# Two softmax attentions in groups of four heads, transposes one head ahead, and a mixer whose branches are interleaved

## The reference, cut to what matters

```
def swa_sink_attention(h, w_q, sinks, w_out, k, v, cos, sin):      # 16 heads of 64, 4 key heads
    q = apply_partial_rope((h @ w_q)...)
    s = einsum(q, k_band) * 64 ** -0.5, -inf outside of the window of 128 keys
    m = maximum(max(s, axis=-1), sink)
    p = exp(s - m)
    probs = p / (sum(p, axis=-1) + exp(sink - m))
    return einsum(probs, v_band).reshape(...) @ w_out

def token_mixer(u, ...):
    rq, rk, rv, rg, c_q, c_kv, k_pe, gate_ret, gate_mla = split(u @ w_in)
    rq, rk = apply_rope(rq), apply_rope(rk)
    y_ret = head_norm(retention(rq, rk, rv))                         # 4 heads, 256 wide, decay by distance
    y_ret = (silu(rg) * y_ret) @ w_ret_o
    # latent attention, 8 heads of 128 + 64 (rotary)
    q = rmsnorm(c_q, q_norm) @ w_uq ;  kv = rmsnorm(c_kv, kv_norm) @ w_ukv
    y_mla = softmax_attention(q, k, v, causal) @ w_mla_o
    merged = sigmoid(gate_ret) * y_ret + sigmoid(gate_mla) * y_mla
    return merged @ w_out
```

## Time and profile before

| | |
|---|---|
| Time, median of three runs (range) | 3529.89 us (3528.61 to 3530.32) |
| The profiled execution's own time | 3529.57 us |
| Its span, first to last instruction | 3527.8 us |
| Mean granted clock of TensorE, as a share of 2.4 GHz | 0.936 |
| TensorE busy | 3154.2 us (89% of the span) |
| VectorE, ScalarE, GpSimd busy | 55%, 47%, 38% |
| Chain that ended last, by engine | PE 45%, issue 28%, DVE 13%, POOL 6%, ACT 6% |
| Weight loads: issue to landing | 3.3 us for 512 KB (882 of them) |

### The profile page before, as it was taken

How to read it: one execution, slowest core, us unless ns; L and a number is a source line. 1 busy time by engine, 2 the same in 40 slices (tenths; PEclk the granted TensorE clock), 3 DMA queues, 4 the chain that set the end, 5 groups by cost and what they waited for, 6 DMA issues and landing times.

```text
span 3527.8 us, 58527 instructions
## 1 busy us (share of the span) xinstructions
PE 3154.2 (89%) x18424; PEld 2797.6 (79%) x18424; DVE 1928.8 (55%) x3054; ACT 1657.1 (47%) x3123; POOL 1337.3 (38%) x1068
## 2 busy tenths in 40 slices
PE   6957999996999987789999779999898788999998
PEld 6756898995777775679999767777777677999997
DVE  7342634019899973234700799999302214555565
ACT  1112576779544441237767874444312214555554
POOL 7200588886455530019978755555000000000000
PEclk6888999999999998699999999999999887999999
DMA  6412454540677742134445128877342222555553
GB/s 222 153 50 93 148 173 161 179 161 0 219 256 256 258 162 84 42 121 171 169 166 184 60 84 279 256 257 242 120 155 95 96 96 84 185 184 186 185 187 132
DMA packets 154591, 556.49 MB, mean 158 GB/s; under 512 B 17024, under 2 KB 19840, under 8 KB 154384
## 3 DMA queue, kind: packets, MB, share of 16 engines
q1 hardware_dynamic: 152288, 551.62, 46.4%
q10 hardware_dynamic: 2224, 3.87, 0.3%
HBM read 554.37 MB, written 1.05 MB: 157 GB/s over the span
## 4 chain that ended last, share of the span: by engine, by line
PE 45%; issue 28%; DVE 13%; POOL 6%; ACT 6%; ACTq 1%; DVEq 1%; POOLq 0%; PEldq 0%
PE bank L634 15%; PE bank L907 11%; PE bank L447 7%; PE bank L925 5%; POOL w_parts L2098 4%; DVE a_parts L1794 4%; PE bank L660 3%; DVE w_parts L1791 3%; ACT hT L1209 3%; DVE h_parts L1791 2%; DVE mean L1802 2%; DVE hT L1802 2%; ACT hT L1205 1%; POOL arena L2137 1%; PE bank L889 1%
## 5 line engine op out<-in xcount | busy, mean ns | idle before, releaser
L2098 POOL TENSOR_TENSOR w_parts<-ring,w_parts 128x512 fp32r<-128x512 f32 x512 | 686.8, 1369 | 646.9 <-ACT w_parts L1169 643.4
L634 PE MATMUL bank<-h_parts,w_parts 128*128 128x256 f32 x6144 | 747.4, 284 | 25.0 <-POOL w_parts L2098 23.0
L634 PEld LDWEIGHTS bank<-h_parts,w_parts 128*128 128x128 f32 x6144 | 743.3, 193 | 29.3 <-POOL w_parts L2098 26.4
L1169 ACT ACTIVATE w_parts<-ring 128x512 fp32r<-128x512 f32 x512 | 319.0, 630 | 196.8 <-PE bank L634 178.1
L2049 DVE TENSOR_TENSOR w_parts<-ring,w_parts 128x512 fp32r<-128x512 f32 x384 | 265.2, 692 | 245.3 <-ACT w_parts L1336 237.3
L660 PE MATMUL bank<-w_parts,a_parts 128*128 128x512 f32 x1536 | 371.8, 398 | 17.1 <-DVE a_parts L1794 17.1
L447 PE MATMUL bank<-hT,ring 128*128 128x256 f32 x1584 | 357.4, 390 | 28.4 <-ACT hT L1100 28.4
L660 PE MATMUL bank<-h_parts,a_parts 128*128 128x512 f32 x1536 | 367.5, 395 | 16.2 <-DVE a_parts L1794 16.2
L907 PEld LDWEIGHTS bank<-h_parts,w_parts 128*128 128x128 f32 x3072 | 375.3, 193 | 5.6 <-issue 3.3
L907 PE MATMUL bank<-h_parts,w_parts 128*128 128x256 f32 x3072 | 376.2, 284 | 2.6 <-DVE w_parts L2049 2.6
L447 PEld LDWEIGHTS bank<-hT,ring 128*128 128x128 f32 x1584 | 308.7, 196 | 77.3 <-issue 31.3
(11 more groups left out here) (310 smaller groups left out, 4294.7 us busy)
## 6 DMA issues: line engine op xcount, KB each, us to landing
ring<-stream SPq DMA_DIRECT2D x882, 512.0 KB, 3.3
arena<-stream SPq DMA_DIRECT2D x168, 512.0 KB, 4.4
arena<-consts ACTq DMA_DIRECT2D x1, 1536.0 KB, 6.1
xT<-xin ACTq DMA_DIRECT2D x1, 1024.0 KB, 5.7
out<-hT SPq DMA_DIRECT2D x4, 256.0 KB, 2.2
arena<-subk ACTq DMA_DIRECT2D x2, 128.0 KB, 2.2
arena<-consts_s ACTq DMA_DIRECT2D x1, 256.0 KB, 2.6
cst<-consts ACTq DMA_DIRECT2D x1, 196.0 KB, 2.6
```

Of the source, the lines that this page charges most:

```text
L634: mm = pe.matmul(bank[k][:, 0:T], w[:, wp, ws], h_parts[:, hp, 4 * j + q, :], start=(j == 0 and q == 0 and i == 0), stop=(j == 1 and q == ...
L1169: act.activation(w_parts[half % HALVES][:, 0, :], ring[slot_][:, j * 512:(j + 1) * 512], ACT.Copy).then_inc(sem(f"{n}_high"), 1)
L2098: pool.tensor_tensor(w[:, 1, :], ring[(base + k) % RING][:, j * 512:(j + 1) * 512], w[:, 0, :].bitcast(F32), ALU.subtract).then_inc(sem(f" ...
```

## The change

- Both attentions: the softmax runs in groups of four heads (`HG`). VectorE masks four heads, takes their maxima and signals; ScalarE takes that group's exponentials meanwhile. The scaling of the probabilities follows in a second loop of VectorE, one group after the other.
- In TensorE's loop over heads the transposes of head h+1 come ahead of the products of head h. The output copies move from VectorE to ScalarE, each behind the copy of the next head's transposes.
- Mixer: the order of the stream becomes `mla_uk`, `mla_uq`, `mla_uv`, `ret_o`. TensorE's order after gate r is: sums of squares of the latents, gate m, retention scores, `mla_uk`, retention products, `mla_uq` with the head means behind its third slot, head variances, `mla_uv`, rotations, wait for `r_yn`, `ret_o` 0 to 3, attention scores, `ret_o` 4 to 7, attention, `mla_o`, `mix_out`. The roots of cq and ckv lie between the two gates on ScalarE, and ahead of the retention scores on VectorE. VectorE multiplies `ret_o` 0 to 3 by the gate ahead of its softmax, 4 to 7 behind it.
- `merged` is made by chunks of 128 features, each behind its `mla_o`; the first `mix_out` projection waits for each chunk ahead of the product that reads it.
- `M.y` gets its own place in memory, and `M.sq` takes that of before.

The diff, cut to its core:

```diff
-    ("gate_r", 8), ("gate_m", 8), ("ret_o", 8), ("mla_uq", 6), ("mla_uk", 2), ("mla_uv", 2), ("mla_o", 8),
+    ("gate_r", 8), ("gate_m", 8), ("mla_uk", 2), ("mla_uq", 6), ("mla_uv", 2), ("ret_o", 8), ("mla_o", 8),
...
         def project(...)
+                if made is not None:
+                    pe.wait_ge(*made(q))
                 mm = pe.matmul(t[:, 0:T], w[:, q * P:(q + 1) * P], src[:, q, :], start=(q == 0), stop=(q == n - 1))
...
+        def attention_pe(pe, n, heads, vcols, vtok):
+            def turned(h):
                 pe.wait_ge(sem(f"{n}_p"), h + 1)
                 t = open_tile(f"{n}_pt{h}")
                 pe.wait_ge(free_sem(f"{n}_pt{h}"), freed(f"{n}_pt{h}") - 1)
                 for k in range(3):
                     mm = pe.transpose(t[:, k * P:(k + 1) * P], A.p[:, h, k * P:(k + 1) * P], ident)
                 mm.then_inc(full_sem(f"{n}_pt{h}"), 1)
+            def weighed(h):
                 pe.wait_ge(free_sem(f"{n}_pt{h}"), freed(f"{n}_pt{h}"))
                 t = open_tile(f"{n}_o{h}")
...
+            turned(0)
+            for h in range(1, heads):
+                turned(h)
+                weighed(h - 1)
+            weighed(heads - 1)
...
         def mix_pe(pe):
             for c in range(8):
                 project(pe, "gate_r", c, hT, f"r_gate{c}")
+            norm_pe(pe, "cq", M.sqc, 3)
+            norm_pe(pe, "ckv", M.sqk, 2)
             for c in range(8):
                 project(pe, "gate_m", c, hT, f"m_gate{c}")
...
+            pe.wait_ge(sem("r_yn"), 1)
+            for c in range(DC // 2):
+                project(pe, "ret_o", c, M.y, f"r_o{c}")
+            scores_pe(pe, "m", MH, scores)
+            for c in range(DC // 2, DC):
+                project(pe, "ret_o", c, M.y, f"r_o{c}")
+            attention_pe(pe, "m", MH, lambda h: slice(h * P, (h + 1) * P), M.vm)
...
-            pe.wait_ge(sem("merged"), 1)
-            project_norm(pe, "mix_out", M.mg, "mix", "2b")
+            project_norm(pe, "mix_out", M.mg, "mix", "2b", lambda q: (sem("merged"), q + 1))
...
+        def attention_act(act, n, heads, sinks):
+            for g in range(heads // HG):
+                act.wait_ge(sem(f"{n}_max"), g + 1)
+                gs = slice(g * HG, (g + 1) * HG)
+                if sinks:
+                    act.activation(A.m[:, :, gs], A.m[:, :, gs], ACT.Exp).then_inc(signal("w_sink"), 1)
+                    act.wait_ge(sem("w_sink"), signalled("w_sink"))
+                for h in range(g * HG, (g + 1) * HG):
...
+        def attention_copies_act(act, n, heads, outp):
+            def out(h):
+                act.wait_ge(full_sem(f"{n}_o{h}"), filled(f"{n}_o{h}"))
+                outp(h, tile_of(f"{n}_o{h}")).then_inc(free_sem(f"{n}_o{h}"), 1)
+                act.wait_ge(free_sem(f"{n}_o{h}"), freed(f"{n}_o{h}"))
             for h in range(heads):
+                if h >= 2:
+                    act.wait_ge(full_sem(f"{n}_o{h - 2}"), filled(f"{n}_o{h - 2}"))
                 copy_act(act, A.pt[:, h % 2, :], f"{n}_pt{h}", lambda t: t[:, 0:384])
+                if h:
+                    out(h - 1)
+            out(heads - 1)
...
         def mix_act(act):
             for c in range(8):
                 copy_act(act, M.gr[:, c, :], f"r_gate{c}", func=ACT.Sigmoid)
+            root_act(act, "cq", rs[:, :])
+            root_act(act, "ckv", G2.r2)
             for c in range(8):
                 copy_act(act, M.gm[:, c, :], f"m_gate{c}", func=ACT.Sigmoid)
+            act.wait_ge(full_sem("r_s3"), filled("r_s3"))
+            for i in range(8):
+                copy_act(act, M.kn[:, i, :], f"m_k{i}")
             for h in range(RH):
                 copy_act(act, M.y[:, 2 * h:2 * h + 2, :], f"r_y{h}", lambda t: t[:, :].rearrange("p (e t) -> p e t", e=2))
+            for i in range(10):
+                copy_act(act, M.qn[:, i, :] if i < 8 else M.qp[:, i - 8, :], f"m_q{i}")
             for h in range(RH):
                 act.wait_ge(sem("r_cent"), h + 1)
                 act.activation(M.sq[:, 2 * h:2 * h + 2, :], M.y[:, 2 * h:2 * h + 2, :], ACT.Square).then_inc(signal("r_sq"), 1)
                 act.wait_ge(sem("r_sq"), signalled("r_sq"))
+            for i in range(10, 12):
+                copy_act(act, M.qp[:, i - 8, :], f"m_q{i}")
             root_act(act, "r", M.r)
...
+        def softmax_dve(dve, n, heads, scale, mask, sinks):
+            for g in range(heads // HG):
+                gs = slice(g * HG, (g + 1) * HG)
+                for h in range(g * HG, (g + 1) * HG):
+                    dve.wait_ge(full_sem(f"{n}_s{h}"), filled(f"{n}_s{h}"))
+                    t = tile_of(f"{n}_s{h}")
+                    dve.scalar_tensor_tensor(A.p[:, h, :], t[:, 0:384], scale, mask, ALU.mult, ALU.add)\
+                       .then_inc(free_sem(f"{n}_s{h}"), 1)
+                dve.tensor_reduce(A.m[:, 0, gs], A.p[:, gs, 0:P], AX.X, ALU.max)
+                dve.tensor_reduce(A.m[:, 1, gs], A.p[:, gs, P:3 * P], AX.X, ALU.max).then_inc(signal("dve_step"), 1)
...
+                    dve.tensor_scalar(A.x[:, :, gs], A.m[:, :, gs], -1.0, None, ALU.mult).then_inc(sem(f"{n}_max"), 1)
+            for g in range(heads // HG):
+                dve.wait_ge(sem(f"{n}_exp"), (g + 1) * HG)
...
+                dve.reciprocal(A.l[:, :, gs], A.l[:, :, gs]).then_inc(signal("dve_step"), 1)
...
+                for h in range(g * HG, (g + 1) * HG):
+                    for b, cols in ((0, slice(0, P)), (1, slice(P, 3 * P))):
+                        ins = dve.tensor_scalar(A.p[:, h, cols], A.p[:, h, cols], A.l[:, b, h:h + 1], None, ALU.mult)
+                    ins.then_inc(sem(f"{n}_p"), 1)
...
+            scale_out(range(DC // 2))
+            softmax_dve(dve, "m", MH, float(192) ** -0.5, c2("mmask"), None)
+            scale_out(range(DC // 2, DC))
             for c in range(DC):
...
                 dve.tensor_tensor(M.gm[:, c, :], t[:, 0:T], M.gm[:, c, :], ALU.mult).then_inc(free_sem(f"m_out{c}"), 1)
                 dve.wait_ge(free_sem(f"m_out{c}"), freed(f"m_out{c}"))
-            dve.tensor_tensor(M.mg, M.gr, M.gm, ALU.add).then_inc(signal("merged"), 1)
+                dve.tensor_tensor(M.mg[:, c, :], M.gr[:, c, :], M.gm[:, c, :], ALU.add).then_inc(sem("merged"), 1)
```

More of the change, by code:

```diff
@@ L55 @@
 NE = NG * EG
+HG = 4
 NEG = -1.0e30
@@ L436, in norm_pe, with project @@
             mm.then_inc(full_sem(f"n{u}_ss"), 1)
-        def project(pe, name, k, src, tile, n=DC, fresh=None):
+        def project(pe, name, k, src, tile, n=DC, fresh=None, made=None):
             w = slot(name, k)
@@ L684, in back_pe, with scores_pe @@
                 square_sum_pe(pe, u, c)
-        def attention_pe(pe, n, heads, scores, vcols, vtok):
+        def scores_pe(pe, n, heads, scores):
             for h in range(heads):
@@ L692, in attention_pe @@
                 mm.then_inc(full_sem(f"{n}_s{h}"), 1)
-            for h in range(heads):
+        def attention_pe(pe, n, heads, vcols, vtok):
+            def turned(h):
                 pe.wait_ge(sem(f"{n}_p"), h + 1)
@@ L766, in mix_pe @@
                 mm.then_inc(full_sem(f"r_s{h}"), 1)
+            pe.wait_ge(sem("m_ckvn"), 2)
+            for k in range(2):
+                w = slot("mla_uk", k)
+                pe.wait_ge(landed_sem("mla_uk", k), landed_at("mla_uk", k))
+                for j in range(4):
+                    t = open_tile(f"m_k{4 * k + j}")
+                    pe.wait_ge(free_sem(f"m_k{4 * k + j}"), freed(f"m_k{4 * k + j}") - 1)
+                    for q in range(2):
+                        mm = pe.matmul(t[:, 0:T], w[:, (2 * j + q) * P:(2 * j + q + 1) * P], M.ckv[:, q, :],
+                                       start=(q == 0), stop=(q == 1))
+                        if j == 0 and q == 0:
+                            mm.then_inc(ring_free, 1)
+                    mm.then_inc(full_sem(f"m_k{4 * k + j}"), 1)
             for h in range(RH):
@@ L1264, in swa_act, with outp @@
                 copy_act(act, S.q[:, c, :], f"w_q{c}")
-            act.wait_ge(sem("w_max"), 1)
-            act.activation(A.m, A.m, ACT.Exp).then_inc(signal("w_sink"), 1)
-            act.wait_ge(sem("w_sink"), signalled("w_sink"))
-            attention_act(act, "w", SH)
-            attention_copies_act(act, "w", SH)
+            attention_act(act, "w", SH, True)
+            def outp(h, t):
+                rows = slice((h % 2) * SHD, (h % 2 + 1) * SHD)
+                return act.activation(A.o[rows, h // 2, :], t[rows, 0:T], ACT.Copy)
+            attention_copies_act(act, "w", SH, outp)
         def mix_act(act):
```

181 lines of the change are left out of this document (63 added, 118 removed).

## The result

| | before | after |
|---|---|---|
| Time, median (range) | 3529.84 us (3528.61 to 3530.32) | 3436.03 us (3433.47 to 3436.47) |
| Ratio, with 95% interval | | 0.9734 (0.9720 to 0.9749) |
| The profiled execution's own time, its span | 3529.57, 3527.8 us | 3433.47, 3431.6 us |
| Mean granted clock | 0.936 | 0.951 |

The changed kernel is 93.8 us faster, by the medians; 3439.4 was forecast, in a range of 3428 to 3456.

The account below looks back on a forecast made before the run. TensorE was busy 89% of the span, so gains lay only in its waits or lower clock. Window attention 40.4, its projection 1.8, mixer 48.1 and `mix_out` 0.2 sum to 90.5 us: 3439.4 us forecast, range 3428 to 3456.

Parts of the forecast that it names:

- Softmax by groups: Window attention's softmax: VectorE paces at 5.1 us per group of four heads; first products start at 1410.3 us.
- Loop: Window attention's loop over heads: 4.5 us at half clock, then 13.7 heads of 1.0 us each.
- The projection's 1.8 us: Projection after the window attention: starts at full clock, its first 48 passes taking 10.4 us instead of 12.17.
- Mixer to the wait: Mixer from the retention scores (2693.90): last variance sum ends 42.1 us later, `ret_o` starts at 2752.1.
- The wait of "some 7 us": Mixer, ahead of `ret_o` 0: a wait of some 7 us remains in place of 11.90 and 6.15.
- Mixer's attention: Mixer: `ret_o` 4 to 7 hide the whole softmax, the loop starts warm, `mix_out` starts 48.1 us earlier.
- Roots between the gates: Mixer: moving the sums of squares between the gates costs 0, or up to 3 us if PSUM cover is short.
- rival 1: Window attention's loop never leaves half clock: 3454 us, chance 0.14.
- rival 2: Hand-over not fully hidden because of ScalarE's single queue, 1.5 us a head at full clock: 3450 us, chance 0.12.
- rival 3: In the attention loops, banks keep transposes from running ahead, heads stay at some 3 us: 3489 us, chance 0.03.
- rival 4: Projections behind the attentions and the retention run at half clock, 110 us in all: 3549 us, chance 0.02.
- Range: Whole kernel: 3428 to 3456 us, including rivals 1 and 2; the forecast's own range was 3430 to 3447.

## Why the prediction was right, step by step

The mechanism held at each step. The sizes were off by 4.0 us one way (window attention) and by 0.2 and 1.3 the other (its projection, the mixer), so they partly cancel: 2.5 us in all, of the 3.4 by which the median lies below the forecast. The rest is not explained by a step.

- **Softmax by groups.** I had first products at mask + 25.6; they came at mask + 22.39. The mis-sized term is VectorE's group of four: 5.1 us in my sum, 4.32 measured. Some 0.5 us of it is that I priced a mask at 0.61 us, a pitch with VectorE's own wait behind each in it, and the two reductions as one after the other, though the diff drops both kinds of wait (four masks now take 1.95 us, 0.49 each, and the second reduction starts 0.08 us before the first one ends). The run with the waits of before puts this at 2.0 us for the four groups. The other 0.27 us a group, 1.1 us in four, is the small steps, taken as 0.7 and measured as 1387.28 - 1386.75 = 0.53, and some 0.1 left over. ScalarE's exponentials follow without a gap, at 4.3 us a group too, so neither engine waits long for the other.
- **Loop.** 18.8 us forecast from the first product to the projection, 18.05 measured. Half clock lasted 3.3 us from the first product where I took 4.5; my bounds were 3.2 and 6.5, and in the run with VectorE's waits put back it lasted 4.8 and the loop took 18.75. A head at full clock takes 1.0 us as forecast. 3.2 + 0.75 are the 4 us by which the window attention gave more (44.35, not 40.4). The projection's 1.8 us were 12.17 - 10.60 = 1.6.
- **Mixer to the wait.** Count from G = 2647.01 - 2.16 = 2644.85, where the retention scores would stand with the squares behind them as before. The last variance sum ends at G + 42.1, as forecast; `ret_o` 0 starts at G + 58.3, forecast 58.2. The wait of "some 7 us" is 6.02 with a small wait of 0.18 behind it; from the fourth rotation's end to `ret_o` 0 it is 7.4, the fifth rotation included. VectorE's first step of the second rotation, which frees the bank, ends it, as forecast. The loss of clock behind it was 1.9 in my sum and 16.32 - 13.98 = 2.3.
- **Mixer's attention.** Scores begin at G + 74.4 (73.9), first products 25.4 later (25.2), `mla_o` 33.9 after the scores begin (33.3), no wait ahead of `mix_out` (0). Together 47.0 us gained in place of 48.3.
- **Roots between the gates.** I took 0, with 3 us as the bound. TensorE's group of 128 passes there is unbroken (27.79 us).
- **Rivals.** The loop left half clock after 3.3 us (rival 1), no head has a pause that ScalarE ends at full clock (rival 2), transposes do run ahead (rival 3), and the projections are at full clock (rival 4), with 2.3 us lost behind the one wait. Rivals 1 and 3 together are nearly what happens with the transposes not ahead: 0.50 for the whole loop, at 2.96 us a head.
- **Range.** The bounds that the prediction lists add up to 6 us below the forecast, 3433.4 and not 3430, and VectorE's group, the term that was off most, had no bound in them. The measured 3436.03 lies inside either way.

What stays open: why half clock lasts 3.3 us in one execution and 4.8 or 5.7 in others, from starts that look alike; no run here separates this.

## What to carry to other kernels

Price an instruction that loses its own wait at the pitch without the wait, from a place in the trace where none stands behind it; I took the pitch of before, which had the wait in it. The busy time of one such instruction is no lower bound either: one mask alone is 0.56 us, and masks in a row came every 0.47. When a wait in a loop goes, price the clock with it: here each head lost 1.0 us to waiting and 0.9 to half clock. And when a latency can't be removed, look for work that only a later step needs and that is about as long as the wait: two projections of 6.9 us in a wait of 6.0 gave 9.2 us, one of 16.8 us in a hole that was already partly hidden gave 4.4.

## What the runs showed of the hardware

- The same loop with the same wait in each head stayed at a granted clock of 0.50 through 46.5 us when it began there, and at 1.00 through its 8 heads when it began at 1.00. The level at which it began decided, not the loop.
- Transposes (32 bit, 128x128) run at the full clock and hold it: 1.00 from 1399 on with nothing else on TensorE, through 4.4 us of them and a wait of 1.43 us. The rise came 2.9 us into them, behind scores without a gap; whether transposes raise the clock without such work ahead no run shows.
- The clock survived waits of 0.66 us in every head and one of 1.43 us; it fell behind one of 2.52 us and one of 3.20 us, when work had begun again, and in one of 6.02 us (0.89 in the stretch from 2698 to 2701.7, 0.50 from 2701.7 on).
- A semaphore wait of VectorE on its own last instruction costs (2.33 - 1.95) / 3 = 0.13 us between two masks of 128x384, and keeps the second reduction from starting before the first has ended. Without it masks overlap: eight in a row took 3.83 us in the run with one group, (3.83 - 0.56) / 7 = 0.47 us each, where one alone takes 0.56.
